# One decoder step: prompt attention's query tiles in another order

## The chip, the cores and the metric

The kernel runs on one core of a Trainium2 chip. The metric is the time of one execution on the device in microseconds, as the median of several runs.

## The reference, cut to what matters

The program computes one inference step of a two-layer decoder trunk for a prompt of 2048 tokens and for 8 sample sequences. Layer 0 mixes tokens by sparse attention, layer 1 by a recurrent block, and each is followed by a mixture of experts. The change touches the prompt's sparse attention alone. What it computes is this, for 16 query heads, 4 key heads, head size 64 and 8 indexer heads:

```
def indexer_scores(qi, wi, ki, q_pos, k_pos):
    dots = jnp.einsum('bqhd,bsd->bqhs', qi, ki)
    s = jnp.einsum('bqhs,bqh->bqs', jax.nn.relu(dots), wi * IDX_SCALE)
    return jnp.where(k_pos <= q_pos, s, -jnp.inf)
...
sc = indexer_scores(qib, wib, ki, q_pos, k_pos)
_, idx = lax.top_k(sc, 256)
valid = idx <= q_pos
return sparse_attend(qb, gather_rows(k, idx), gather_rows(v, idx), valid)
```

Each of the 2048 queries picks the 256 earlier keys with the highest indexer score and attends to these. The queries are handled in 16 blocks of 128, and no block needs another's result.

## The kernel before, in words

The kernel is a row of phases, one after the other: modulation, projection, prompt attention (`phase_attend`), sample attention, routing, experts, the recurrent layer, and the second layer's experts. Only prompt attention depends on the list `TILE`, which has one entry for each block of 128 queries. Tile t sees the keys 0 to 128(t+1)-1, so its width is L = 128(t+1) columns: 128 for tile 0, 2048 for tile 15.

Nothing is gathered. For each tile the kernel does four things, one stage apart:

- **Index** (TensorE L1046, ScalarE L763, VectorE L841 and L845): for each of 8 indexer heads and each cut of at most 512 columns one unit of work: a product, a relu, a multiply and add into `score`. That is I = 8 x cuts units.
- **Search** (`pieces_at`, 37 pieces): a search bit by bit for the value of the 256th largest score. For tiles with L of at least 1024 (7 to 15, `by_act`), each of 31 rounds is a sign over the whole width on ScalarE (`weigh`, L768) and two small VectorE instructions (L866, L868) that set the next candidate. The next sign waits for them. For tiles 2 to 6 VectorE counts alone (L853, L911, L913). Tiles 0 and 1 need no search, as all their keys are taken. Then VectorE writes `hide` over the width (L932 to L944).
- **Fill** (`fill`, `largest`): for each of 16 heads and each cut one unit: two TensorE products into one of two PSUM banks (L1006, L1007) and a maximum over it on VectorE (L811). That is U = 16 x cuts units. The third unit must wait until VectorE has read the first.
- **Attend**: S = 4(t+1) blocks of 128 keys for 4 heads each, two in a slot: bias and score (L978, L985), exponential on ScalarE (L731), product with the values (L996). Then the sums are copied (L741), inverted (L824), multiplied (L827) and projected by `w_out` (L1018), one stage later, in that stage's middle slot.

The loop over i = -3 to 16 attends tile TILE[i] while it fills for TILE[i+1], searches for TILE[i+2] and indexes for TILE[i+3]. A stage has S/2 slots, so 2(t+1) of them, by the tile that is attended. The fills are spread over the slots ahead of the middle one, the index pairs over the middle and the later slots, and the search pieces over all but the last, with double weight ahead of the middle. Inside a slot the order on each engine is written out: TensorE does bias and score, the first half of the slot's fills, the value product of the slot before, and the other fills; ScalarE does the two exponentials, then relus, then the slot's signs; VectorE does the slot's maxima, the normalising of the tile before, index adds, and the slot's search pieces. At i = -3 to -1 nothing is attended, there is one slot, and everything of the stage stands in it.

Of the kernel before, what the change touches and what calls it, by code (L numbers as in the profile page):

```python
# [29 lines left out]
NT = SEQ // P  # L30
# [453 lines left out]
def phase_attend(nc, T):  # L484
# [7 lines left out]
    with ExitStack() as ctx, Semaphores(nc, T["whole_run"], ("y_out",)) as sems:  # L492
# [49 lines left out]
             "y_out", "consts", "spare"))  # L542
        crossed, split_done, asked, balanced = (sem(n) for n in ("crossed", "split_done", "asked", "balanced"))

        TILE = [0] + list(range(1, NT, 2)) + list(range(NT - 2, 0, -2))
        L = [P * (t + 1) for t in TILE]
        CUTS = [-(-l // 512) for l in L]
        U = [H * c for c in CUTS]
        I = [IH * c for c in CUTS]
        S = [NKV * (t + 1) for t in TILE]  # L550
        PIECES = 37
# [72 lines left out]
        def rows_at(m):  # L624
            return slice(TILE[m] * P, TILE[m] * P + P)

# [2139 lines left out]
def build(nc, T):  # L2766
    with ExitStack() as stack:
# [8 lines left out]
        with ExitStack() as attention:  # L2776

            keep("KT", [P, NKV // 2, SEQ], until=attention)
            keep("kiT", [P, SEQ], until=attention)
            keep("V1", [P, NT, NKV, P], until=attention)  # L2780
            with ExitStack() as projecting:
                keep("project_w", [P, KC, C_END], until=projecting)
                phase_modulation(nc, T)
                phase_project(nc, T)
            phase_attend(nc, T)
# [83 lines left out]
```

## Time and profile before

| what | value |
|---|---|
| median of 3 runs | 6136.24 us (6133.54 to 6142.34) |
| the profiled execution's own time | 6147.33 us |
| its span | 6145.7 us |
| granted TensorE clock, mean of the span | 0.853 of full speed |
| prompt attention's stages, from its first instruction to its last copy (L741) | 660.0 to 2884.3 us of the span |

The span runs from the first to the last instruction. In the trace's rows a time is in us from the span's start unless it is marked ns, and "idle before <-" names what an engine waited for. PEclk 1.00 is TensorE at 2.4 GHz, 0.50 at 1.2 GHz, and a mean between them says how much of a stretch had each.

### The profile page before, as it was taken

Reading aid. Unit: us, or ns where it says so; the run is one execution under the profiler, and the core shown is the slowest. Engines: PE = TensorE matmul, PEld = TensorE weight load, DVE = VectorE, ACT = ScalarE, POOL = GpSimd, SP = SyncE. Lnnn points to the kernel's source line nnn. Section 1 sums busy time; section 2 is a strip of 40 time slices with the busy share of each in tenths; the row PEclk is TensorE's granted clock in tenths of the full one; section 3 lists DMA queues with packets and bytes.
Section 4 is the critical chain, followed back from the end, with each engine's and each line's share of the span. In section 5 each row is a group of like instructions: output and inputs, shape, how many; then the busy total and the mean of one; then the engine's idle time right before and its main releaser. Section 6 shows DMA issues by size and latency. Waiting matters only on the chain. (4 is left out here: it accounts for less than half of the span.)

```text
span 6145.7 us, 54949 instructions
## 1 busy us (share of the span) xinstructions
PE 4685.9 (76%) x15814; PEld 2443.1 (40%) x15868; DVE 2258.1 (37%) x5087; ACT 1825.2 (30%) x3166; POOL 659.1 (11%) x798
## 2 busy tenths in 40 slices
PE   7999545667788998887744999828788785589980
PEld 2444112222333333333334444316556554444430
DVE  1111374444555545662524001054434442411105
ACT  0111124556565655222111122212222321112212
POOL 0111210000001000011021000120000000100013
PEclk9999667788999999999865999959898885589995
DMA  6111100000000000000535777560010001347865
GB/s 250 53 52 43 56 21 12 12 6 12 7 13 13 13 13 13 13 11 24 195 121 215 278 279 265 214 251 21 20 41 21 20 21 41 128 171 270 290 240 192
DMA packets 153248, 603.55 MB, mean 98 GB/s; under 512 B 24576, under 2 KB 27008, under 8 KB 134121
## 3 DMA queue, kind: packets, MB, share of 16 engines
q1 hardware_dynamic: 97946, 407.29, 18.7%
q0 software_dynamic: 34208, 119.30, 5.5%
q10 hardware_dynamic: 20928, 75.00, 3.0%
q8 instruction: 75, 1.23, 0.1%
q14 instruction: 91, 0.74, 0.0%
HBM read 466.97 MB, written 134.61 MB: 98 GB/s over the span
## 5 line engine op out<-in xcount | busy, mean ns | idle before, releaser
L2190 PE MATMUL experts_ps_gu<-w_sb,experts_xT 128*128 x1504 | 677.5, 604 | 45.9 <-DMA w_sb<-moe_w_in 41.4
L996 PE MATMUL attend_po<-attend_PT,V 128*128 128x512 f32 x1088 | 572.3, 652 | 9.0 <-ACT attend_total L741 9.0
L768 ACT ACTIVATE attend_passed<-attend_score,attend_cand 128x1024 bf16<-128x1024 f32 (+8 forms) x279 | 439.3, 1575 | 356.9 <-DVE attend_cand L868 333.2
L2707 PE MATMUL recurrent_psAB<-recurrent_hT,rec_w_in_sb 128*128 128x256 f32 (+1 forms) x2304 | 536.1, 392 | 10.6 <-ACT recurrent_hT L2502 10.6
L468 PE MATMUL project_pj<-project_w,project_hT 128*128 128x512 f32 (+2 forms) x1360 | 507.8, 531 | 6.6 <-ACT project_proj L384 5.5
L2707 PEld LDWEIGHTS recurrent_psAB<-recurrent_hT,rec_w_in_sb 128*128 128x128 f32 x2304 | 463.6, 215 | 77.0 <-issue 11.8
L811 DVE TENSOR_REDUCE attend_mx<-attend_aux 128x1 f32<-128x512 f32 (+3 forms) x640 | 365.0, 606 | 278.5 <-PE attend_aux L1007 271.5
L2190 PEld LDWEIGHTS experts_ps_gu<-w_sb,experts_xT 128*128 128x128 f32 x1504 | 284.3, 194 | 374.1 <-issue 374.1
L1006 PE MATMUL attend_aux<-attend_hide,attend_identb 128*128 128x512 bf16 (+3 forms) x587 | 223.7, 384 | 244.2 <-DVE attend_mx L811 231.5
L731 ACT ACTIVATE attend_PT<-attend_big 128x512 f32<-128x512 f32 x544 | 292.5, 589 | 366.1 <-PE attend_big L985 365.4
L2180 PE MATMUL experts_ps_y<-w_sb,experts_midT 128*128 x752 | 343.0, 599 | 11.4 <-issue 11.4
L468 PEld LDWEIGHTS project_pj<-project_w,project_hT 128*128 128x128 f32 (+1 forms) x1360 | 229.5, 185 | 261.9 <-issue 254.8
L985 PE MATMUL attend_big<-attend_qT,KT 64*128 64x512 f32 x1088 | 333.5, 692 | 0.0
L996 PEld LDWEIGHTS attend_po<-attend_PT,V 128*128 128x128 f32 x1088 | 209.4, 205 | 275.0 <-issue 205.7
L2144 DVE SCALAR_TENSOR_TENSOR experts_th<-experts_th,experts_ps_gu 128x256 f32<-128x256 f32 x94 | 39.6, 421 | 735.5 <-ACT experts_th L2123 735.5
L1006 PEld LDWEIGHTS attend_aux<-attend_hide,attend_identb 128*128 128x128 bf16 x640 | 64.9, 102 | 579.9 <-DVE attend_mx L811 445.1
L1046 PE MATMUL attend_aux<-kiT,attend_qiT 64*128 64x512 f32 (+3 forms) x640 | 183.0, 654 | 142.2 <-ACT attend_relu L763 111.7
L1007 PE MATMUL attend_aux<-attend_KTb,attend_qTb 128*128 128x512 bf16 (+3 forms) x640 | 241.4, 383 | 57.2 <-POOL attend_qTb L708 42.2
L2738 PE MATMUL recurrent_psO<-rec_w_out_sb,recurrent_g 128*128 128x512 f32 (+1 forms) x544 | 240.1, 602 | 28.9 <-DVE recurrent_g L2664 28.9
L1018 PE MATMUL attend_aux<-attend_w_out,attend_oT 128*128 128x512 f32 x512 | 227.7, 603 | 20.5 <-DVE attend_oT L827 20.5
L845 DVE SCALAR_TENSOR_TENSOR attend_score<-attend_relu,attend_wi,attend_score 128x512 f32<-128x512 f32 (+3 forms) x280 | 185.4, 670 | 143.3 <-ACT attend_relu L763 126.5
L2123 ACT ACTIVATE experts_th<-experts_ps_gu 128x256 f32<-128x256 f32 x94 | 36.1, 384 | 679.9 <-PE experts_ps_gu L2190 679.9
(465 smaller groups left out, 5793.4 us busy)
## 6 DMA issues: line engine op xcount, KB each, us to landing
w_sb<-moe_w_in SPq DMA_DIRECT2D x64, 2048.0 KB, 11.7
w_sb<-moe_w_in SPq DMA_DIRECT2D x64, 1024.0 KB, 8.5
yb_scratch<-experts_y ACTq DMA_DIRECT2D x94, 512.0 KB, 8.3
index_slab<-ada_w_in SPq DMA_DIRECT2D x12, 2048.0 KB, 9.7
route_x<-xa_scratch SPq DMA_DIRECT2D x32, 512.0 KB, 4.6
hs_scratch<-route_h ACTq DMA_DIRECT2D x32, 512.0 KB, 4.8
yb_scratch<-route_blank SPq DMA_DIRECT2D x32, 512.0 KB
combine_x<-xa_scratch SPq DMA_DIRECT2D x32, 512.0 KB, 4.6
```

The lines of the kernel that those rows point to most:

```text
L468: last = pe.matmul(pj[0:rows, bank, 0:c1 - c0], hT[:, b, k, 0:rows], w[:, k, c0:c1], start=(k == 0), stop=(k == KC - 1))
L731: act.activation(PT[:, g % 4, :], big[:, g % 4, :], ACT.Exp).then_inc(exped, 1)
L768: act.activation(passed[:, 0:L[m]], score[:, m % 2, 0:L[m]], ACT.Sign, bias=threshold, accum_out=balance[:, :]).then_inc(balanced, 1)
L811: dve.tensor_reduce(mx[:, h, c:c + 1], aux[:, u % 2, 0:wide], AX.X, ALU.max).then_inc(maxed, 1)
L985: pe.matmul(big[:, g % 4, :], KT[r, n // 2, b * P:(b + 1) * P], qT[r, i % 3, n // 2 * GQ:(n // 2 + 1) * GQ, :].rearrange("p a q -> p (a q) ...
L996: pe.matmul(po[:, n % 2, :], V1[:, b, n, :], PT[:, g % 4, :], start=(b == 0), stop=(b == S[i] // NKV - 1)).then_inc(pv_done, 1)
L1006: pe.matmul(aux[:, u % 2, 0:n], identb4[:, 0, :], hide[:, keys], start=True, stop=False)
L1007: pe.matmul(aux[:, u % 2, 0:n], qTb[:, h, :], KTb[:, h // GQ // 2, keys], start=False, stop=True).then_inc(unit_filled, 1)
L2180: last = pe.matmul(ps_y[:, half, :], midT[:, k, :], w2[:, bass.ds(slot, 1), k, half * 512:half * 512 + 512].rearrange("p a n -> p (a n)"), ...
L2190: last = pe.matmul(ps_gu[:, u, :], xT[:, u, k, :], w1[:, bass.ds(slot, 1), k, :].rearrange("p a n -> p (a n)"), start=(k == 0), stop=(k == ...
L2707: last = pe.matmul(psAB[:, c % 2, part, 0:W], w_in[:, k, part * D + c * P:part * D + (c + 1) * P], hT[:, k, 0:W], start=(k == 0), stop=(k ...
L2738: last = pe.matmul(psO[0:rows, half, :], g[:, k, i * P:i * P + rows], w_out[:, k, half * 512:half * 512 + 512], start=(k == 0), stop=(k == ...
```

## The change

The list gets another order. Nothing else is edited.

```
-        TILE = [0] + list(range(1, NT, 2)) + list(range(NT - 2, 0, -2))
+        RAMP = [1, 4, 8, 12]
+        TILE = RAMP + [t for t in range(NT - 1, -1, -1) if t not in RAMP]
```

Before, TILE is 0, 1, 3, 5, 7, 9, 11, 13, 15, 14, 12, 10, 8, 6, 4, 2. After, it is 1, 4, 8, 12, 15, 14, 13, 11, 10, 9, 7, 6, 5, 3, 2, 0. L, CUTS, U, I and S are worked out from it.

## Rows read from the trace of the kernel before

**Rows 1.** The page's first line.

```profile
span 6145.7 us, 54949 instructions
```

**Rows 2.** Busy time by stretch: length, engines' busy us, PEclk, DMA share, GB/s.

```profile
660.00:726.10 66.10, 28.30 (x109) 13.70 (x110) 18.85 (x53) 12.91 (x31) 24.43 (x21) 0.50 0.30 104
726.10:805.80 79.70, 27.32 (x97) 10.28 (x96) 56.75 (x174) 15.23 (x33) 6.66 (x6) 0.59 0.04 10
805.80:911.40 105.60, 59.32 (x157) 22.35 (x156) 81.52 (x178) 23.23 (x47) 12.39 (x9) 0.74 0.05 18
911.40:1054.90 143.50, 83.55 (x253) 32.71 (x253) 61.05 (x150) 67.66 (x125) 13.62 (x9) 0.77 0.04 13
1054.90:1207.30 152.40, 102.19 (x298) 38.27 (x300) 71.90 (x155) 80.20 (x133) 14.28 (x9) 0.80 0.04 12
1207.30:1392.20 184.90, 129.27 (x395) 49.02 (x398) 81.69 (x174) 93.23 (x149) 14.41 (x9) 0.80 0.03 10
1392.20:1567.10 174.90, 137.71 (x442) 51.41 (x444) 90.57 (x179) 105.34 (x157) 15.07 (x9) 0.89 0.03 11
1567.10:1759.50 192.40, 155.22 (x521) 61.47 (x525) 95.15 (x191) 114.56 (x165) 15.49 (x9) 0.91 0.03 10
1759.50:1938.00 178.50, 159.28 (x569) 62.67 (x574) 96.48 (x192) 113.20 (x173) 15.92 (x9) 0.97 0.03 11
1938.00:2111.40 173.40, 162.17 (x600) 67.64 (x604) 89.75 (x188) 108.10 (x173) 15.72 (x9) 0.98 0.03 11
2111.40:2273.10 161.70, 149.29 (x577) 63.90 (x581) 80.88 (x185) 97.66 (x169) 15.30 (x9) 0.99 0.03 12
2273.10:2416.20 143.10, 131.12 (x482) 55.42 (x486) 69.74 (x160) 84.87 (x153) 14.87 (x9) 0.98 0.04 14
2416.20:2561.00 144.80, 120.31 (x433) 49.86 (x436) 94.77 (x210) 39.27 (x83) 14.52 (x9) 0.93 0.04 13
2561.00:2681.00 120.00, 99.69 (x339) 41.03 (x341) 76.06 (x186) 32.60 (x67) 14.01 (x9) 0.93 0.04 14
2681.00:2782.00 101.00, 78.07 (x271) 32.37 (x273) 60.86 (x177) 24.71 (x50) 14.03 (x9) 0.93 0.06 21
2782.00:2842.00 60.00, 52.77 (x187) 22.61 (x185) 16.47 (x24) 20.36 (x42) 12.93 (x9) 1.00 0.05 18
2842.00:2884.30 42.30, 36.55 (x110) 15.02 (x108) 7.81 (x5) 16.64 (x38) 5.28 (x3) 1.00 0.07 25
```

**Rows 3.** The timeline in the stage of tile 3: two signs in a row.

```profile
932.06 1.15 ACT L768 ACTIVATE attend_passed<-attend_score,attend_cand 128x1024 bf16<-128x1024 f32 x1 [0.46 <-DVE attend_cand L868]
...
933.75 1.15 ACT L768 ACTIVATE attend_passed<-attend_score,attend_cand 128x1024 bf16<-128x1024 f32 x1 [0.46 <-DVE attend_cand L868]
```

**Rows 4.** One line's instructions, durations ns min/median/max: ScalarE's signs, VectorE's counts.

```profile
L768 ACT ACTIVATE attend_passed<-attend_score,attend_cand x279: 1147/1575/2002, 927.0 to 2385.5; 128x1024 bf16<-128x1024 f32 x16, 128x1536 bf16<-128x1536 f32 x16, 128x2048 bf16<-128x2048 f32 x16, 128x1664 bf16<-128x1664 f32 x16
...
L853 DVE TENSOR_SCALAR_CACHE_REDUCE attend_passed<-attend_score,attend_cand x169: 611/879/2346, 742.1 to 2756.7; 128x512 bf16<-128x512 f32 x32, 128x768 bf16<-128x768 f32 x32, 128x896 bf16<-128x896 f32 x32, 128x640 bf16<-128x640 f32 x32
```

**Rows 5.** The timeline in early slots of the stages of tiles 3, 7 and 9.

```profile
936.08 0.61 PE L1006 MATMUL attend_aux<-attend_hide,attend_identb 128*128 128x512 bf16 x1 [9.53 <-DVE attend_mx L811]
...
1228.29 3.62 PE L996 MATMUL attend_po<-attend_PT,V 128*128 128x512 f32 x4
...
1414.47 1.88 PE L996 MATMUL attend_po<-attend_PT,V 128*128 128x512 f32 x4
```

**Rows 6.** VectorE's timeline at the end of tile 7's search.

```profile
1044.00 1.28 DVE L853 TENSOR_SCALAR_CACHE_REDUCE attend_passed<-attend_score,attend_cand 128x1024 bf16<-128x1024 f32 x1
...
1051.34 0.43 DVE L944 TENSOR_SCALAR attend_hide<-attend_hide 128x1024 bf16<-128x1024 bf16 x1
```

**Rows 7.** The timeline before the first attended tile: two index units of tile 3.

```profile
714.46 2.08 PE L1046 MATMUL attend_aux<-kiT,attend_qiT 64*128 64x512 f32 x4 [1.17 <-ACT attend_relu L763]
```

**Rows 8.** The timeline in the last stage: inverting and projecting.

```profile
2848.38 6.59 DVE L824 RECIPROCAL attend_total<-attend_total 128x256 f32<-128x256 f32 x4 [35.98 <-ACT attend_total L741]
...
2857.10 13.90 PE L1018 MATMUL attend_aux<-attend_w_out,attend_oT 128*128 128x512 f32 x32
```

## The prediction, made before the changed kernel was run

> **What bounds the kernel now.** I took the length of the whole first [rows 1], then cut prompt attention into its stages by the busy times of stretches [rows 2], and only then looked into single slots with the timeline [rows 3, 5 to 8] and at one line's durations [rows 4]. The reader is to see in rows 2 that the 17 stretches (the preparation i = -3 to -1, then one stage for each tile) add up to 2224.3 us, and that they are of two kinds. In the stages of tiles 15, 14 and 12, TensorE is busy 162.2 of 173.4, 149.3 of 161.7 and 131.1 of 143.1 us at a clock of 0.98 to 0.99: TensorE bounds them. In the stages of tiles 0 to 9 on the way up it is busy 34 to 79% at a clock of 0.59 to 0.89: no engine is full there, and the chain of dependences is what takes the time. The change cannot alter the sum of the work (every tile is indexed, searched, filled and attended once, and all instructions and DMAs are the same, on the same queues); it alters only which parts lie beside each other. All outside the attention phase stays, 6145.7 - 2224.3 = 3921.4 us [rows 1, 2].
>
> I write a stage as attended/filled/searched/indexed tile. Its parts are:
> - **rounds**: two signs of tile 7 start 1.69 us apart with a sign of 1.15 us [rows 3], so a round is its sign plus 0.54. Signs run from 1.15 us (1024 columns) to 2.00 (2048) [rows 4]; by the straight line between, a round takes 1.70 us for tile 7, 1.80 (8), 1.91 (9), 2.01 (10), 2.12 (11), 2.23 (12), 2.34 (13), 2.44 (14) and 2.55 (15). A VectorE count runs from 0.61 us up [rows 4]; with 0.5 for its small instructions I take 1.11 (tile 2), 1.25 (3), 1.38 (4), 1.51 (5), 1.65 (6). Thirty-one of them.
> - **tail** of the search: 1044.0 to 1051.8 = 7.8 us for tile 7 [rows 6], and some 3 for its last checks: 11 us, and 2 more for every 256 columns. VectorE's searches: 5 to 9.
> - **fills** 1.1 us each (0.9 to 1.0 where a cut of 128 columns is among them), **index** 0.98, both fitted below; **projection** 16 (13.9 at full clock [rows 8]) and 6 for joining two stages.
>
> **If nothing overlapped**, 3/5/7/9 would take 53 + 11 + 32 x 1.1 + 24 x 0.98 + 22 = 144 us; it takes 143.5. 5/7/9/11: 59 + 13 + 36 + 24 + 22 = 154 against 152.4. 7/9/11/13: 66 + 15 + 50 + 31 + 22 = 184 against 184.9 [rows 2]. So in stages of up to 16 slots search and fills simply follow each other, and the attended tile's own work costs nothing. From 20 slots on they overlap: 9/11/13/15 sums to 196 and takes 174.9, 11/13/15/14 to 219 and takes 192.4, 13/15/14/12 to 217 and takes 178.5. Rows 5 show why: with 5 fills or fewer in a slot two stand ahead of the value product, both find a free bank, and the product (1.88 us) runs under the signs; with 6 or more the third fill waits for VectorE (9.53 us) and the product comes after the search, at half clock (3.62 us).
>
> **The change part by part.** Before, eight stages (tiles 0 to 13) climb to tile 15; after, four do, but each searches a tile far wider than the one it attends.
> - Preparation, 66.1 us now. Indexing tiles 1, 4, 8 in place of 0, 1, 3 is 48 units for 24; at half clock a pair of full units costs 3.25 us (2.08 + 1.17 [rows 7]), so 16 more full units are 26 and 8 more narrow ones some 5. Tile 4's search has nothing beside it: 31 x 1.38 + 7 = 50, less the 6 us of joining that go on under it; the wider fills of tile 1 add 2. Sum 143 (136 to 149). As tile 1's first bias waits for no search, it may stand ahead of tile 4's search in the trace; then these 50 us are seen in tile 1's stage.
> - 1/4/8/12 (4 slots): 56 + 12 + 32 x 0.9 + 32 x 1.1 (index at half clock) + 7, no projection = 139. With the index at 0.98 and less for the narrow fills it is 131; at 3.25 for each pair, 156.
> - 4/8/12/15 (10 slots): 69 + 16 + 46 + 32 + 22 = 185 (178 to 196).
> - 8/12/15/14 (18 slots): 79 + 19 + 62 + 31 + 22 = 213. With 7 fills in a slot the product stays exposed, so I take no overlap; with what 20 slots gave, 21, it is 192.
> - 12/15/14/13 (26 slots, 4 or 5 fills in each): between 192.4 and 178.5, nearer the latter: 180.
> - TensorE-bound ones, from their neighbours at 5.5 us a slot: 15/14/13/11 175, 14/13/11/10 168, 13/11/10/9 155.
> - 11/10/9/7 140 and 10/9/7/6 135: from 12/10/8/6 (143.1) 11 us less for every two slots, 8 and 6 more since the same rounds stand in fewer slots.
> - VectorE's searches don't overlap: 10/8/6/4 sums to 143 and takes 144.8, 8/6/4/2 to 116 and takes 120.0. So 9/7/6/5: 51 + 9 + 37 + 15 + 22 + 3 = 137, 7/6/5/3 123, 6/5/3/2 109, 5/3/2/0 92.
> - Ends: 3/2/0 is 4/2 (60.0) less two slots, 53; 2/0 44 (42.3 now, and 16 small fills); then tile 0 alone. Its two slots hide nothing: copies 3 us twice, inverting and multiplying 8 (6.59 + 1.23), projection 14 [rows 8], waits 9 = 37.
>
> The sum is 143 + 139 + 185 + 213 + 180 + 175 + 168 + 155 + 140 + 135 + 137 + 123 + 109 + 92 + 53 + 44 + 37 = 2228 us against 2224.3: **4 us more**, so 6151 us for an execution like the profiled one (6147.3), which stood 0.18% above the median of the runs. On the median it is 6140 us. Before, the preparation and the climb (tiles 0 to 13) took 1278.0 us and the rest 946.3; after, the preparation and four stages take 860 and the other twelve 1368. So the shorter climb saves 418 us, and the seven stages that move to the way down cost as much, since the waste of the climb sits in the searches, which are all still there: tile 4's lies bare, and three of the widest (8, 12, 15) meet short stages.
>
> **Rivals.**
> 1. *The stage's own work gives the overlap: the old ramp's idle time goes.* At the 5.4 us a slot of tile 15's stage (173.4 / 32 [rows 2]) the eight climbing stages with their 114 slots would take 616 us, and they took 1212. If each new stage lost only what an old one attending a tile of its size lost over this, the parts give 1/4/8/12 126, 4/8/12/15 168, 8/12/15/14 188, 12/15/14/13 178, 10/9/7/6 131: 61 us less in all, 6079. For it: 9/11/13/15 is shorter than 7/9/11/13 with more work. Against it: the two preceding it obey the plain sum. Chance 0.12.
> 2. *Partial overlap.* 8/12/15/14 with 18 slots overlaps like 20 slots (-21) and the index of 1/4/8/12 runs at 0.98 (-8): 6140 - 29 = 6111. For it: 16 slots none, 20 slots 21, nothing says where between the step is. Chance 0.20.
> 3. *The other side: the clock.* The coarse new stages leave TensorE idle longer than the old ones, so index and projection run at 1.2 GHz in them. The granted clock was 0.50, 0.59, 0.74, 0.77, 0.80 in the first five stretches [rows 2], rising with the slots. If the three coarse stages stay near 0.6, 32 index units each in two of them at 1.62 (3.25 a pair) for 0.98 is 41 at most, of which VectorE's own work hides half, and two projections, 13.9 each at full clock [rows 8], add 5 each: about +30, 6170. What speaks for it is that a TensorE wait of 9.5 us under 6 or 7 rounds [rows 5] becomes one of some 25 us under the 14 rounds in a slot of 1/4/8/12; what speaks against it, that 8/12/15/14 has the rounds in a slot of 7/9/11/13. It decides if the clock there is under 0.65. Chance 0.26. The Trainium skill, "TensorE: Matmul & The Clock Gate", section "Loop structure matters more than you think", says that whether matmuls stay at full clock is set by the loop nest, and that a long wait before each makes them run at the lower one. By that rule the new coarse stages get the lower clock, and this rival's +30 holds in place of my +4; rows 2 agree in kind, for the earliest, coarsest stages have the lowest clock.
>
> The forecast itself (within some 12 us of 6140) has 0.42.
>
> **How the numbers follow.** The low bounds of the preparation and of the first four stages (-7, -8, -7, -21, -2), with some -10 for the others, won't all come together: 6140 - 38 = 6102 takes in rival 2 and leaves out rival 1. The high ones are +6, +17, +11, +5, +6 and 10 for the rest; two thirds of them give 6176, with rival 3 inside. A measurement of this kernel tells about 0.2% (12 us) from no change. Faster than 6124 are rivals 1 and 2, 0.32; slower than 6148 is rival 3 and a small part of my own case, 0.28; 0.40 is left between.
>
> **What would show it.** In the changed kernel's stretches: tile 4's search with TensorE idle for some 45 us ahead of tile 4's fills; 139 (without that search), 185 and 213 us for the stages of tiles 1, 4 and 8 at a clock below 0.8; value products of 3.6 us there; a clock of 0.97 or more from tile 12 to tile 11; tile 4's stage beginning at about 942 us of the span, tile 15's at about 1520. I am wrong if the stage of tile 8 is under 200 us (rival 2), if all three coarse stages are 10% shorter (rival 1), or if they are longer with a clock under 0.65 (rival 3).

## The result, and the profile after

The changed kernel takes 6155.68 us (median of 12 runs, 6146.96 to 6158.76) against 6135.82 (12 runs, 6130.34 to 6142.34) on the same chip: 1.003 times the time before, with a 95% interval of 1.0021 to 1.0039. So it is 0.3% slower, some 20 us, where 4 were forecast. It lies in the range and beyond the 12 us that were to count as no change.

The page's first line of the changed kernel:

```profile
span 6157.1 us, 55002 instructions
```

The changed kernel's busy times by stretch, cut at the first bias product of each attended tile: length, busy us of PE, PEld, DVE, ACT and POOL, then PEclk, DMA share, GB/s. In order: preparation, then tiles 1, 4, 8, 12, 15, 14, 13, 11, 10, 9, 7, 6, 5, 3, 2, 0.

```profile
659.50:756.40 96.90, 47.44 (x155) 18.70 (x156) 36.72 (x76) 23.38 (x55) 24.72 (x21) 0.55 0.21 71
756.40:950.80 194.40, 60.64 (x185) 21.68 (x184) 101.86 (x290) 66.44 (x115) 7.30 (x6) 0.58 0.01 4
950.80:1137.60 186.80, 107.85 (x327) 39.77 (x326) 83.42 (x178) 92.29 (x137) 14.24 (x9) 0.77 0.03 10
1137.60:1350.70 213.10, 144.57 (x454) 55.17 (x453) 94.28 (x191) 109.47 (x153) 15.30 (x9) 0.83 0.03 9
1350.70:1528.50 177.80, 156.14 (x550) 59.58 (x549) 98.07 (x193) 112.32 (x169) 15.92 (x9) 0.96 0.03 11
1528.50:1701.70 173.20, 162.51 (x607) 66.58 (x606) 90.87 (x185) 111.56 (x173) 15.72 (x9) 1.00 0.03 11
1701.70:1868.60 166.90, 155.36 (x583) 64.85 (x582) 86.05 (x185) 102.70 (x169) 15.50 (x9) 0.98 0.04 12
1868.60:2020.70 152.10, 142.02 (x527) 59.29 (x526) 78.03 (x169) 96.39 (x165) 15.08 (x9) 0.99 0.04 13
2020.70:2159.60 138.90, 125.18 (x463) 52.03 (x461) 71.25 (x160) 86.88 (x149) 14.87 (x9) 0.99 0.04 14
2159.60:2293.20 133.60, 117.98 (x438) 49.27 (x437) 66.90 (x161) 77.58 (x145) 14.66 (x9) 0.97 0.04 14
2293.20:2427.60 134.40, 109.56 (x383) 45.01 (x382) 92.41 (x195) 37.95 (x79) 14.28 (x9) 0.95 0.04 14
2427.60:2547.60 120.00, 93.17 (x319) 37.69 (x318) 81.36 (x186) 31.40 (x63) 14.07 (x9) 0.93 0.05 16
2547.60:2657.40 109.80, 85.13 (x295) 35.54 (x294) 69.13 (x187) 28.36 (x59) 13.79 (x9) 0.92 0.05 17
2657.40:2750.80 93.40, 72.29 (x239) 30.41 (x237) 56.72 (x171) 24.38 (x55) 13.37 (x9) 0.89 0.05 18
2750.80:2809.10 58.30, 50.70 (x170) 21.56 (x169) 18.29 (x26) 18.19 (x38) 12.93 (x9) 0.94 0.10 36
2809.10:2862.00 52.90, 41.33 (x139) 17.80 (x138) 12.85 (x24) 16.01 (x34) 11.71 (x9) 0.90 0.06 20
2862.00:2900.50 38.50, 26.02 (x62) 10.20 (x60) 7.81 (x5) 12.21 (x30) 5.26 (x3) 0.87 0.04 10
```

These answer to [rows 2]. They add up to 2241.0 us against 2224.3: prompt attention is 16.7 us longer. The engines' work is as it was (DVE 1146.0 us against 1150.3, ACT 1047.5 against 1049.8), so the 16.7 us are waiting. The rest of the span, which the change doesn't touch, is 3916.1 us against 3921.4; in the profiles of all kernels here it lies between 3901 and 3921 us, so these 5 us are noise of single executions. Preparation and climb went from 1278.0 to 869.0 us (forecast 860), and the other stages grew from 946.3 to 1372.0 (forecast 1368). From tile 12 down to tile 10 TensorE is busy 88 to 94% of the time, at a clock of 0.96 to 1.00.

Two places in the changed kernel's timeline hold most of what was not forecast. The first is the index in tile 1's stage, early in it and late in it. In a row stand start, length, engine and line, and in brackets the idle time before; an index row with x4 holds two units. The first row is the first fill for tile 4: ahead of it TensorE stands idle for 48.70 us, which is tile 4's search with nothing beside it.

```profile
808.48 0.59 PE L1007 MATMUL attend_aux<-attend_hide,attend_identb 128*128 128x512 bf16 x1 [48.70 <-issue]
...
900.16 2.08 PE L1047 MATMUL attend_aux<-kiT,attend_qiT 64*128 64x512 f32 x4 [1.17 <-ACT attend_relu L764]
903.41 2.08 PE L1047 MATMUL attend_aux<-kiT,attend_qiT 64*128 64x512 f32 x4 [1.17 <-ACT attend_relu L764]
...
944.44 1.13 PE L1047 MATMUL attend_aux<-kiT,attend_qiT 64*128 64x512 f32 x4 [1.17 <-ACT attend_relu L764]
946.74 1.13 PE L1047 MATMUL attend_aux<-kiT,attend_qiT 64*128 64x512 f32 x4 [1.17 <-ACT attend_relu L764]
```

Busy times around both:

```profile
896.00:915.00 19.00, 11.71 (x26) 3.53 (x28) 6.79 (x12) 6.71 (x14) 0.00 (x0) 0.50 0.00 0
...
932.00:950.00 18.00, 7.84 (x24) 2.88 (x24) 12.90 (x18) 5.34 (x12) 0.00 (x0) 0.73 0.00 0
```

At 1.2 GHz (PEclk 0.50) a pair of full units starts every 3.25 us, and later in the stage, where two products together take 1.13 us in place of 2.08, every 2.30. The wait for ScalarE's relu, 1.17 us, is the same at both. The fills differ likewise. These are the maxima over a pair of them (512 and 128 columns) in slots 0 and 1 of the same stage, each with its wait for TensorE:

```profile
811.35 0.89 DVE L812 TENSOR_REDUCE attend_mx<-attend_aux 128x1 f32<-128x512 f32 x2 [0.93 <-PE attend_aux L1008]
...
858.84 0.89 DVE L812 TENSOR_REDUCE attend_mx<-attend_aux 128x1 f32<-128x512 f32 x2 [0.50 <-PE attend_aux L1008]
```

The other place is the stage of tile 2 (2809.1 to 2862.0), on VectorE's timeline and in TensorE's projection:

```profile
2823.50 3.36 DVE L825 RECIPROCAL attend_total<-attend_total 128x256 f32<-128x256 f32 x2
...
2830.99 3.36 DVE L825 RECIPROCAL attend_total<-attend_total 128x256 f32<-128x256 f32 x2
2834.43 1.74 DVE L828 TENSOR_TENSOR attend_oT<-attend_oT,attend_total 128x1024 f32<-128x1024 f32 x1
...
2836.31 15.51 PE L1019 MATMUL attend_aux<-attend_w_out,attend_oT 128*128 128x512 f32 x32 [3.01 <-DVE attend_oT L828]
```

The stage has three slots ahead of its middle. Sixteen small maxima for tile 0 and tile 3's inverting share VectorE there, in written order, and the projection waits for the last of them. It starts 27.2 us after the stage. Before, tile 2 came last with no fills behind it, the inverting ran beside the slots (6.59 us), and the projection started 15.1 us after the stage (2857.10 [rows 8] less 2842.0 [rows 2]).

### The profile page after: what moved, and what is told of

Its sections match the earlier page's. It is cut to its first block and busy times, and to the rows that moved or that the text cites. A ratio compares the mean times of both kernels' runs of the same rounds, so it can differ in the third digit from the quotient of the medians.

```text
span 6157.1 us, 55002 instructions
## 1 busy us (share of the span) xinstructions
PE 4674.4 (76%) x15867; PEld 2438.0 (40%) x15868; DVE 2253.2 (37%) x5087; ACT 1823.0 (30%) x3166; POOL 662.3 (11%) x798
## 5 line engine op out<-in xcount | busy, mean ns | idle before, releaser
L769 ACT ACTIVATE attend_passed<-attend_score,attend_cand 128x1152 bf16<-128x1152 f32 (+8 forms) x279 | 439.3, 1575 | 396.2 <-DVE attend_cand L869 311.9
L1007 PE MATMUL attend_aux<-attend_hide,attend_identb 128*128 128x512 bf16 (+3 forms) x640 | 243.8, 384 | 348.1 <-DVE attend_mx L812 247.2
```

The costliest lines, as they stand in the source:

```text
L769: act.activation(passed[:, 0:L[m]], score[:, m % 2, 0:L[m]], ACT.Sign, bias=threshold, accum_out=balance[:, :]).then_inc(balanced, 1)
L1007: pe.matmul(aux[:, u % 2, 0:n], identb4[:, 0, :], hide[:, keys], start=True, stop=False)
```

## The experiments

Each was compared with the kernel before on its chip. Seven were run. Four read the theory of the prediction (short stages are the plain sum of search, fills, index and projection) from different sides: one more term in the sum, another place for tile 0, no climb, and a climb of one step. Three move the value product.

**extra_sign.** The changed order, and one more sign in each round:

```
 act.wait_ge(asked, asked_of(m) + r + 1)
+act.activation(extra[:, :], score[:, m % 2, 0:448], ACT.Sign, bias=threshold)
 act.activation(passed[:, 0:L[m]], score[:, m % 2, 0:L[m]], ...)
```

> The changed order; ahead of each of the 31 signs of a search on ScalarE stands one more over 448 columns into a buffer of its own, about 0.67 us by the line through the signs' durations. Theory A: it stands in full in the stages where nothing overlaps, so +21 us each in the stages of tiles 1, 4 and 8 (searches of 8, 12 and 15); in the stages of tiles 12 to 10 part of it, 5 to 15 us each, less the closer TensorE is to full; nothing in the stages of tile 9 and later, whose searches are VectorE's. Rival B (partial overlap in all stages of over 4 slots): under 12 us in the stages of tiles 4 and 8.

It took 6256.63 us (one run), with a span of 6254.7. Its stretches for tiles 1, 4, 8 and 12:

```profile
755.80:967.80 212.00, 62.50 (x186) 22.64 (x186) 102.16 (x291) 83.75 (x146) 7.29 (x6) 0.56 0.01 4
967.80:1171.70 203.90, 109.19 (x325) 39.59 (x324) 82.30 (x175) 109.60 (x168) 14.23 (x9) 0.75 0.03 9
1171.70:1397.40 225.70, 147.56 (x455) 55.18 (x453) 94.05 (x192) 126.76 (x184) 15.29 (x9) 0.80 0.03 9
1397.40:1586.80 189.40, 160.19 (x551) 61.49 (x550) 98.66 (x193) 129.49 (x200) 15.92 (x9) 0.94 0.03 10
```

The added sign took 0.67 us, as expected, but the next one started 0.58 us after it, and a round grew by 0.56 us (tile 8's from 1.80 to 2.36), so 31 rounds are 17.4 us. The stage of tile 1 grew by 17.6 and that of tile 4 by 17.1: all of it, so their searches lie on the path from the first round to the last. Tile 8's grew by 12.6, between what theory A and rival B wanted, and tile 12's by 11.6. Tile 15's, which I had taken to be bound by TensorE, grew by 12.1 too (173.2 to 185.3), and those of 14 to 10 by 8 to 11. Tiles 9 to 5 moved by -0.2 to 2.2. So the search is in the plain sum in full up to 10 slots, and with 18 slots a quarter of it is hidden already. And "TensorE-bound" was too strong: a stage in which TensorE is 94% busy still grew by two thirds of what the rounds grew. Part of this is the clock: in tile 15's stage it went from 1.00 to 0.97, and TensorE's own busy time from 162.5 to 167.7 us, 5.2 of the 12.1.

**tile0_first.** `RAMP = [0, 1, 4, 8, 12]` in place of `[1, 4, 8, 12]`; the order ends in 3, 2.

> Tile 0 goes from the end of the order to its front: 0, 1, 4, 8, 12, 15, 14, ..., 3, 2. Theory A (short stages are the plain sum of their search, fills, index and projection, whatever the attended tile): the preparation and the stages of tiles 0 and 1 take some 71 + 99 + 164 = 334 us where preparation and tile 1 took 291.3, so +43; the end loses the stage of tile 0 (38.5) and the stages of tiles 3 and 2 go back from 58.4 and 52.8 to some 53 and 42, with 5 less for tile 5's: -59. Net -16: prompt attention about 2225 us, 6139 us in all. Rival B (tile 4's bare search is the loss, and a stage beside it hides it): the stage of tile 0 costs no more than the 79.7 us that it cost in the kernel before, and the net is -40: 6116 us. Rival C (the clock: what is short and idle runs at 1.2 GHz): one more short stage at the front, 10 to 20 us more than A says: 6150 to 6160 us.

It took 6140.76 us (11 runs), 1.0014 times the kernel before (1.0005 to 1.0023). Its stages of tiles 0 and 1, and then those of tiles 3 and 2 (the preparation took 71.2 us):

```profile
731.90:826.10 94.20, 34.66 (x113) 12.33 (x112) 65.94 (x181) 18.70 (x41) 6.65 (x6) 0.57 0.03 9
826.10:983.90 157.80, 78.78 (x223) 30.03 (x222) 64.67 (x160) 70.50 (x125) 12.59 (x9) 0.65 0.04 12
...
2787.30:2844.30 57.00, 49.41 (x163) 20.93 (x162) 16.36 (x24) 18.17 (x38) 12.90 (x9) 0.94 0.06 19
2844.30:2888.30 44.00, 38.20 (x110) 15.41 (x108) 7.83 (x6) 16.63 (x38) 5.27 (x3) 0.96 0.07 24
```

The front costs 323.2 us against 291.3 (+31.9, expected +43), and the end, tile 5's stage included (92.1), 193.1 against 243.1 (-50.0, expected -59). Prompt attention is 2227.6 us, 13.4 less than with the changed order and 3.3 more than before. So of the 16.7 us that the change cost, most hang on where tile 0 stands. The rival by which a stage beside tile 4's search would hide it is out: it wanted -40. So is the rival of the clock, which wanted the front longer than the sum said; it was 11 us shorter.

**down_from_15.** `RAMP = [0, 1]`: no climb at all.

> No climb: 0, 1, 15, 14, 13, ..., 3, 2. Theory A: preparation 105, tile 0's stage (fills of 1, search of 15, index of 14) 162, tile 1's (fills of 15, search of 14, index of 13) 229, then 174, 168, 157, 146, 140, 135, 128, 135, 129, 115, 108, 86, 53, 42 down to tile 2: 2212 us of prompt attention against 2241 with the changed order, so about 6127 us. Rival C (the clock): the first two stages, with 32 index units and 64 fills at 1.2 GHz, take 40 us more than A says, and the gain over the changed kernel is gone: 6160 to 6170 us. Rival D (a stage's length goes by the attended tile): tiles 0 and 1 cost what they cost before, 80 and 106, and it falls to about 6000 us.

It took 6128.89 us (11 runs), 0.9994 times the kernel before (0.9985 to 1.0003): the same within the interval. The first three stretches:

```profile
659.50:764.40 104.90, 52.71 (x154) 19.29 (x155) 35.66 (x75) 25.96 (x55) 24.48 (x21) 0.50 0.19 66
764.40:922.90 158.50, 47.00 (x130) 14.74 (x129) 59.49 (x142) 89.46 (x111) 6.66 (x6) 0.54 0.02 5
922.90:1130.20 207.30, 104.92 (x286) 32.20 (x285) 99.20 (x192) 91.25 (x125) 14.93 (x9) 0.69 0.03 9
```

Expected were 105, 162 and 229, and 2212 us in all; it is 2217.4. The total is close because two misses cancel: tile 1's stage came out 21.7 us under its sum, and the later stages together some 31 over theirs. The sum charged 1.1 us for each of the 64 fills of that stage. In its trace the 32 maxima of the first slot take 24.2 us (929.35 to 953.55), 0.76 each, and the last 16 of them 0.69. As an estimate, 0.76 in place of 1.1 on 64 fills is 21.8 us, the size of the miss:

```profile
942.52 11.03 DVE L812 TENSOR_REDUCE attend_mx<-attend_aux 128x1 f32<-128x512 f32 x16 [1.46 <-PE attend_aux L1008]
```

What the 1.1 held besides is told below, under the price of a fill. Tile 0's stage, two slots long, took 158.5 us, where it took 79.7 before [rows 2]: the searched and indexed tiles set its length, and the attended one doesn't. The clock rival wanted 40 us more than the sum and got none.

**climb_by_8.** `RAMP = [0, 1, 8]`.

> The order 0, 1, 8, 15, 14, ..., 2, fills as in the kernel before. Theory A by its plain sums: preparation 85, tile 0's stage (search of 8, index of 15 at half clock) 134, tile 1's (fills of 8, search of 15, index of 14) 207, tile 8's (fills of 15, search of 14, index of 13) 212, then as measured in down_from_15 and tile0_first: 2249 us of prompt attention, 25 more than before. Rival (a climb with fewer steps always gains, since each climbing stage wastes the same): under 2225 us.

One run, 6151.92 us; prompt attention is 2244.3 us, the sum had said 2249. The stretches of tiles 0, 1 and 8 against 134, 207 and 212 (the preparation took 84.2 for 85):

```profile
745.00:877.00 132.00, 49.43 (x130) 14.89 (x129) 53.10 (x139) 67.17 (x111) 6.65 (x6) 0.54 0.02 6
877.00:1076.70 199.70, 90.28 (x252) 31.16 (x253) 84.03 (x176) 95.40 (x125) 13.44 (x9) 0.65 0.03 10
1076.70:1287.30 210.60, 147.67 (x450) 55.01 (x454) 98.01 (x190) 105.32 (x153) 15.93 (x9) 0.84 0.03 9
```

Fewer climbing stages don't gain by themselves: with tiles 0 and 1 first, a climb of none gives 2217.4 us, one by tile 8 2244.3, one by 4, 8 and 12 2227.6. Why the single step is the worst of the three was not looked into.

**two_ahead.** The changed order; the fills ahead of the value product are capped at two:

```
+ahead = min(2, len(units) // 2)
-for u in units[:len(units) // 2]:
+for u in units[:ahead]:
     fill(i + 1, u)
 ...
-for u in units[len(units) // 2:]:
+for u in units[ahead:]:
     fill(i + 1, u)
```

> The changed order; of a slot's fills only two, not half of them, stand ahead of the value product on TensorE. Theory A with the row of the third fill that waits for VectorE: with 6 or more fills in a slot (tiles 1, 4 and 8 attended) the product now runs under the signs, and each slot but a stage's first saves up to its 3.5 us: 1 + 4 + 8 slots, 30 to 45 us less, 6111 to 6126 us; the stages from tile 12 on, with 5 fills or fewer, stay within 2 us. Rival: the product is not on the path, since the exponentials and the later fills wait for VectorE anyway: within 5 us of the changed kernel.

It took 6121.78 us (11 runs), 0.9986 times the kernel before (0.9977 to 0.9995). Its stretches for tiles 4, 8 and 12:

```profile
953.10:1132.30 179.20, 113.65 (x326) 39.56 (x325) 83.13 (x176) 92.27 (x137) 14.22 (x9) 0.75 0.03 11
1132.30:1324.90 192.60, 140.59 (x454) 52.17 (x454) 94.29 (x192) 109.43 (x153) 15.32 (x9) 0.85 0.03 10
1324.90:1502.60 177.70, 156.15 (x548) 59.51 (x548) 98.06 (x193) 112.25 (x169) 15.91 (x9) 0.96 0.03 11
```

Tile 8's stage fell from 213.1 to 192.6 us, tile 4's from 186.8 to 179.2, and tile 12's, which never had a third fill ahead, stayed at 177.7 (177.8). Tile 1's, with its one product to gain, didn't move (195.3 against 194.4). Prompt attention is 2210.6 us, 30.4 less. Besides the 28.1 of tiles 8 and 4, tile 15's stage is 2.6 us longer and those of tiles 3 and 2 are 3.4 and 3.2 us shorter. In tile 3's the order of the instructions is the same in both kernels; it shows what the clock alone does there (58.3 us at 0.94 in the changed kernel):

```profile
2728.50:2783.40 54.90, 47.31 (x170) 20.65 (x169) 18.20 (x26) 18.17 (x38) 12.92 (x9) 1.00 0.11 39
```

In the slots one sees the product leave the path. In the changed kernel, and then in this one, in tile 8's stage:

```profile
1169.52 0.61 PE L1007 MATMUL attend_aux<-attend_hide,attend_identb 128*128 128x512 bf16 x1 [4.80 <-DVE attend_mx L812]
...
1170.35 3.55 PE L997 MATMUL attend_po<-attend_PT,V 128*128 128x512 f32 x4
...
1174.37 1.49 DVE L812 TENSOR_REDUCE attend_mx<-attend_aux 128x1 f32<-128x512 f32 x3 [3.09 <-PE attend_aux L1008]
```

```profile
1168.99 1.88 PE L997 MATMUL attend_po<-attend_PT,V 128*128 128x512 f32 x4
...
1174.33 1.48 DVE L812 TENSOR_REDUCE attend_mx<-attend_aux 128x1 f32<-128x512 f32 x3
```

Above, TensorE waits 4.80 us with the third fill, then runs the product in 3.55 us, and VectorE waits 3.09 us for the next fill. Below, the product starts 5 us ahead of the next maxima, in 1.88 us, and they wait for nothing. So the product is on the path, and the rival is out. The Trainium skill ("PSUM — Partial Sum Buffer", section "Engine vs sequencer instructions") says that matmuls start and complete in program order. The traces agree: the third fill's wait of 4.80 us held back the product, which didn't need what the fill needed.

**two_ahead_before.** The same edit with the order of the kernel before.

> The order of the kernel before, with two fills ahead of the value product in each slot. Theory A, with what two_ahead showed (tile 8's stage, 7 fills in a slot, 213.1 to 192.6; tile 4's, 9 or 10 fills, 186.8 to 179.2; stages with 5 or fewer unchanged): the stage of tile 7 (6 fills, 8 slots) loses some 20 us, tile 3's (8 fills, 4 slots) 6, tiles 5 and 11 with every third slot at 6 fills 4 and 8; all others within 2. Together 38 us: ratio to before 0.994. Rival: what two_ahead gained belongs to searches of the widest tiles alone; then tile 7's stage, which searches tile 11, loses less than 8, and the whole less than 15.

It took 6088.88 us (5 runs), 0.9924 times the kernel before (0.9911 to 0.9937), the fastest of all. Its stretches for tiles 3, 7, 11 and 13:

```profile
911.10:1048.20 137.10, 82.92 (x252) 32.06 (x253) 61.41 (x151) 67.63 (x125) 13.56 (x9) 0.77 0.04 14
...
1197.60:1363.20 165.60, 124.99 (x394) 47.19 (x397) 82.76 (x175) 93.09 (x149) 14.46 (x9) 0.85 0.03 12
...
1535.80:1716.60 180.80, 148.62 (x521) 58.27 (x525) 94.46 (x191) 114.63 (x165) 15.53 (x9) 0.94 0.03 11
1716.60:1896.50 179.90, 160.95 (x568) 63.23 (x573) 97.03 (x193) 113.14 (x173) 15.98 (x9) 0.95 0.03 11
```

The stages of tiles 3, 7 and 11 are 6.4, 19.3 and 11.6 us shorter (expected 6, 20 and 8), and tile 13's, which has no slot with six fills, is 1.4 us longer. Prompt attention is 2179.7 us, 44.6 less where 38 were expected. The gain belongs to the number of fills in a slot, wherever that stage stands.

**two_ahead_tile0.** Both edits: `RAMP = [0, 1, 4, 8, 12]` and two fills ahead.

> The order 0, 1, 4, 8, 12, 15, 14, ..., 3, 2 with two fills ahead. Theory A: the two edits touch different stages and add up: tile0_first's prompt attention of 2227.6 us less the 28 of tiles 4 and 8, so 2199 us, ratio to before 0.997; slower than two_ahead_before by some 12 us. Rival (a common cause, the clock, so that the second edit brings less): over 2210 us.

It took 6111.62 us (6 runs), 0.996 times the kernel before (0.9948 to 0.9973); prompt attention is 2203.1 us, 4 more than the two effects together and under the 2210 of the rival. Both orders have gained from the cap. The order of before stays 23 us ahead, where 12 were expected.

## Why the prediction was right, and where its sizes were off

The range held the time, and the main account held: the shorter climb moves the searches and doesn't remove them. The likeliest case did not come: between 6124 and 6148 us had 0.40, and what came is slower, to which 0.28 was given. The sign was that of the forecast, the size was not. Of the signs named ahead, TensorE's idle time ahead of tile 4's fills (48.7 us for some 45), the value products (3.55 for 3.6) and the starts of tile 4's and tile 15's stages (950.8 for 942, 1528.5 for 1520) came; the clock in tile 8's stage was 0.83, where under 0.8 was named.

- **Stages of tiles 4, 8 and 12.** Forecast 185, 213 and 180 us, measured 186.8, 213.1 and 177.8. The plain sum, fitted on three stages of the kernel before, held, and extra_sign shows for tiles 1 and 4 that the search is on the path in full. For tile 8 the same run shows that a quarter of a longer round is hidden, so that its 213.1 is not a plain sum with nothing beside it; the fitted terms took that in. Rival 2 wanted 192 there and 131 for tile 1's stage, and rival 1 188: both are out.
- **The price of a fill.** The prediction said that up to 16 slots the attended tile's own work costs nothing, and summed tile 7's stage to 184 us without a term for the value product. That was wrong, and the sum was right by its fit. two_ahead_before took 19.3 us out of this very stage by moving the product alone. Over its 48 fills that is 0.40 us each, and without it the 1.1 that I charged for a fill would be 0.70, near the 0.69 to 0.76 that down_from_15 shows; this is an estimate from these two runs. The 1.1 thus holds only where slots have the fills and products of the stages that it was fitted on. The changed kernel's stages of tiles 4 and 8, with 9 or 10 and 7 fills in a slot, are near these (6 to 8). Tile 1's stage in down_from_15, with 32 in a slot, is not, and there the sum gave 21.7 us too much.
- **Preparation and tile 1.** Forecast 143 + 139 = 282 us, measured 96.9 + 194.4 = 291.3. As foreseen, the first bias stands ahead of tile 4's search and its time is seen in tile 1's stage. The 9.3 us divide into three: the preparation took 96.9 us where 143 less the search's 50 is 93, tile 4's search took 52 (756.4 to 808.5) for 50, and the rest of tile 1's stage 142.3 for 139. In that rest the fills of slot 0, at half clock, take 1.82 us for two (0.91, where I took 0.9). The index I had at 1.1 a unit. At half clock a pair of full units takes 3.25 us, 1.62 a unit, but a pair of the 128-column ones only 1.33 (906.65 to 907.98): slot 2's sixteen units, the first from 896.91 and the last ended by 918.45, took 21.5 us where 1.1 each is 17.6. That is 3.9 us for the clock, read from the trace; no run took the low clock away. This is the part of rival 3, the clock, that came true: 0.58 in this stage where rows 2 had 0.74 in tile 1's. The rest of rival 3 did not come: tiles 4 and 8 had 0.77 and 0.83 and were at most 1.8 us beyond the sum.
- **The rule on the loop nest** ("TensorE: Matmul & The Clock Gate" in the Trainium skill, section "Loop structure matters more than you think") is borne out in kind. The page's example is a wait for DMA, and here it is a wait for a search: of the stages that attend a tile, tile 1's, with a wait of 48.7 us, had the lowest clock, 0.58. Its price in the index was about 4 us and not 30. Most of what runs in that stage is rounds on ScalarE and VectorE: tile 8's, in this stage, start 1.80 us apart.
- **The end.** Forecast 53 + 44 + 37 = 134 us for tiles 3, 2 and 0, measured 58.3 + 52.9 + 38.5 = 149.7. This step failed most, by 15.7 us: 5.3 in tile 3's stage, 8.9 in tile 2's and 1.5 in tile 0's. For tile 3's, two_ahead gives most of it: the same instructions in the same order took 54.9 us at a clock of 1.00 and 58.3 at 0.94, so 3.4 of the 5.3 go with the clock. Tile 2's I had priced as the last stage of before (42.3 [rows 2]) plus a little for small fills. In its place the trace shows fills, maxima and inverting in turn ahead of the projection, which starts 12.1 us later in the stage than before (27.2 against 15.1) and takes 15.51 us in place of 13.90. tile0_first shows the size: without tile 0 at the end this stage takes 44.0 us, and the last ones together, tile 5's included, 50.0 less, while tile 0 at the front costs 31.9. How the 12.1 us divide between VectorE's order, TensorE's fills and a wait of 3.50 us ahead of the first of them was not separated.
- **The descent.** From tile 15 to tile 7 I forecast 1033 us (175, 168, 155, 140, 135, 137, 123) and got 1019.1; 13.9 us less, 1.1 to 3.0 in each. No run looked for the cause.
- **The sum.** +9.3 (preparation and tile 1), +1.8, +0.1, -2.2 (tiles 4, 8, 12), -13.9 (15 to 7), +2.2 (6 and 5) and +15.7 (the end) is +13.0, on a forecast of +4: 16.7 us measured. Errors of both signs partly cancelled, and a forecast of a small difference between two sums of 2200 us is no better than that.
- **The 418 us.** The prediction said that the shorter climb saves 418 us and the longer descent costs as much. Measured: 409.0 saved, 425.7 paid.

## What to carry to other kernels

Where a stage of a software pipeline is too short to hide the chains that stand in it, its length is close to the sum of those chains, and reordering the stages moves the waste and doesn't remove it: five orders here lie between 2217 and 2244 us. What removed a part of it (44.6 us with the order of before) was an order inside a slot: an instruction that must wait (a fill whose bank is still being read) was standing on an in-order engine ahead of one that could run. So count how many buffers are free, put only that many of the waiting kind first, and the ready work next. And price the last stages of a pipeline by the chains that now stand in them, not by their own work alone. A term that was fitted on stages of one kind can hold another term's cost: the fill's 1.1 us held the product's wait.

## What the runs showed of the hardware that was not expected

One more sign over 448 columns made a round 0.56 us longer and stretched a stage in which TensorE was 94% busy (162.5 of 173.2 us) by 12.1 us; the granted clock fell from 1.00 to 0.97 there, with 5.2 us more of busy time. A busy share of 94% at full clock did not mean that the chain beside it was free. The same instructions of tile 3's stage took 58.3 us at a mean clock of 0.94 and 54.9 at 1.00, while TensorE's waits for other engines were the same (3.5, 2.4, 1.2 and 0.5 us). And pairs of index units of the same size started 3.25 us apart at 1.2 GHz and 2.30 us apart later in the same stage, their wait for ScalarE's relu being 1.17 us at both.
